# A ring of six value pages and a re-timed order of slots in a two-layer decoder's merged attention stage

## The reference, cut to what matters

```python
# prompt, one block of 128 queries
sc = einsum('bqhd,bkhd->bhqk', qi, k) * scale + ci[..., :, None] - c_k[:, :, None, :]
p = softmax(where(causal, sc, NEG_INF)); out = einsum('bhqk,bkhd->bqhd', p, v)
# sample
k_past = k_pool[page_table].reshape(bd, p_len, h, d)      # v_past, lf_past alike
s_past = einsum('bqhd,bkhd->bhqk', q, k_past) * scale + cq[..., :, None] + r_past
p = softmax(concatenate([s_past, s_new], -1))
out = einsum(p[..., :p_len], v_past) + einsum(p[..., p_len:], v)
```

## Time and profile before

| | us |
|---|---|
| median of 3 runs (lowest, highest) | 2018.95 (2005.68, 2023.38) |
| the profiled execution | 2022.65 |
| its span, first to last instruction | 2020.9 |
| merged stage in it, 1119.0 to 1519.3 | 400.3 |
| of which slots 4 to 27, 1165.4 to 1456.6 | 291.2 |

### The profile page before, as it was taken

How to read it: one execution, slowest core, us unless ns; L and a number is a source line. 1 busy time by engine, 2 the same in 40 slices (tenths; PEclk the granted TensorE clock), 3 DMA queues, 4 the chain that set the end, 5 groups by cost and what they waited for, 6 DMA issues and landing times.

```text
span 2020.9 us, 37879 instructions
## 1 busy us (share of the span) xinstructions
PE 1770.0 (88%) x15111; PEld 1542.6 (76%) x15111; DVE 942.3 (47%) x1367; ACT 561.5 (28%) x1008; POOL 111.4 (6%) x217
## 2 busy tenths in 40 slices
PE   5999565979999999899977687788779899999999
PEld 4876443979999999889954444444439799999998
DVE  5388776453333322467546755555523533333221
ACT  3210223232222211243332333433322322222211
POOL 1000000000000000144310000000000000000000
PEclk9999876999999999999977788888879899999999
DMA  3211031212222322223343677777772222222331
GB/s 118 60 46 32 21 100 42 82 54 83 83 83 80 88 87 86 66 68 79 80 149 98 220 237 246 270 252 254 248 245 69 62 83 83 83 82 82 95 101 53
DMA packets 240211, 224.87 MB, mean 111 GB/s; under 512 B 12290, under 2 KB 200340, under 8 KB 240090
## 3 DMA queue, kind: packets, MB, share of 16 engines
q1 hardware_dynamic: 229776, 201.13, 31.8%
q0 software_dynamic: 8896, 18.79, 3.1%
q10 hardware_dynamic: 1418, 3.29, 0.5%
HBM read 215.37 MB, written 7.80 MB: 110 GB/s over the span
## 4 chain that ended last, share of the span: by engine, by line
PE 76%; DVE 12%; DMA 4%; issue 3%; ACT 3%; SPq 2%; ACTq 0%; DVEq 0%; POOL 0%; POOLq 0%
PE ps L1490 56%; PE ps L1920 4%; DMA vring<-in_cache_fox_v_dram 4%; PE ps L1696 3%; PE ps L1965 2%; PE ps L1899 1%; DVE tmp L440 1%; PE ps L1472 1%; DVE yc L719 1%; SPq L2078 1%; DVE aL L444 1%; DVE rb L435 1%; DVE rb L450 1%; PE ps L1558 1%; PE ps L1881 1%
## 5 line engine op out<-in xcount | busy, mean ns | idle before, releaser
L1490 PE MATMUL ps<-aH,wH 128*128 128x288 f32 x2224 | 488.5, 302 | 49.1 <-DVE aL L444 33.5
L1490 PE MATMUL ps<-aL,wH 128*128 128x288 f32 x2224 | 481.4, 298 | 0.0
L1490 PE MATMUL ps<-aH,wL 128*128 128x288 f32 x2224 | 481.0, 298 | 0.0
L1490 PEld LDWEIGHTS ps<-aH,wH 128*128 128x128 f32 x2224 | 362.7, 191 | 58.0 <-issue 35.6
L421 DVE TENSOR_TENSOR wL<-raw,wH 128x1024 fp32r<-128x1024 f32 (+1 forms) x179 | 232.0, 1296 | 331.9 <-ACT wH L1046 328.8
L1490 PEld LDWEIGHTS ps<-aL,wH 128*128 128x128 f32 x2224 | 363.5, 191 | 0.0
L1490 PEld LDWEIGHTS ps<-aH,wL 128*128 128x128 f32 x2224 | 363.3, 191 | 0.0
L1046 ACT ACTIVATE wH<-raw 128x1024 fp32r<-128x1024 f32 (+1 forms) x179 | 198.9, 1111 | 381.4 <-PE ps L1490 352.2
L1490 PE MATMUL ps<-gH,wH 128*128 128x288 f32 x704 | 151.6, 296 | 0.0
L1490 PE MATMUL ps<-gH,wL 128*128 128x288 f32 x704 | 151.1, 295 | 0.0
L1490 PE MATMUL ps<-gL,wH 128*128 128x288 f32 x704 | 151.0, 295 | 0.0
(11 more groups left out here) (307 smaller groups left out, 1802.3 us busy)
## 6 DMA issues: line engine op xcount, KB each, us to landing
kset<-in_cache_fox_k_dram SPq DMA_DIRECT2D x128, 384.0 KB, 4.3
vring<-in_cache_fox_v_dram SPq DMA_DIRECT2D x128, 384.0 KB, 4.8
raw<-in_w_gate_up_dram SPq DMA_DIRECT2D x88, 512.0 KB, 3.8
raw<-in_w_down_dram SPq DMA_DIRECT2D x32, 704.0 KB, 4.6
raw<-in_fox_w_in_dram SPq DMA_DIRECT2D x21, 512.0 KB, 3.9
raw<-in_w_out_dram SPq DMA_DIRECT2D x16, 512.0 KB, 4.2
raw<-in_conv_w_in_dram SPq DMA_DIRECT2D x14, 512.0 KB, 3.8
raw<-in_w_mem_kv_dram SPq DMA_DIRECT2D x8, 512.0 KB, 3.7
```

What stands on the lines that cost most here:

```text
L1490: mm = nc.tensor.matmul(ps[:, 2 * slot + h, 0:HT], weights[:, w], a[:, k0 + k, h * HT:(h + 1) * HT], start=(first and k == 0 and weights i ...
```

## The change

It alters the merged stage alone. The ring holds six value pages in place of four; the room comes from the buffer qr, so that `spread` now copies straight from qkT, in 16 copies of 32 partitions in place of 4 of 128, and the 16 copies that filled qr ahead of the stage are left out. SP asks for a chunk of keys one slot later. Even slots take three value pages and odd slots five. A sample's transposed probabilities go through banks 0 to 3, which the scores have left, in place of four PT entries of banks 6 and 7; one semaphore (pt_ready) tells ACT of all of them, and the next `set_scores` waits for ACT's copies (pt_taken). On PE `set_scores` and two value pages come ahead of `step_probT`, and `step_values` comes after all of the slot's pages; `step_hi` and `step_lo` treat the step before the last. The two rows of keys' sums (ncb) are made in two slots.

```diff
-    VRING = 4
+    VRING = 6
...
-    TURNS = [("ncb", 0, 0), ("ncb", 0, 1)]
+    TURNS = [("ncb", 0, 0)]
     for s in range(SLOTS + SPB):
         b, cc = divmod(s, SPB)
         step = 1 <= s <= STEPS
-        TURNS += [("probT", s - 1)] if step else []
         if cc == 2 and s < SLOTS:
             TURNS += [("new", b)]
+        TURNS += [("probT", s - 1)] if step else []
         if cc == 1 and b >= 2:
             TURNS += [("out", b - 2)]
+        if s % 5 == 0 and s < STEPS:
+            TURNS += [("ncb", s // 5, 1)]
         TURNS += [("pv", s - 1)] if step else []
-        if cc == 3 and s < SLOTS:
-            TURNS += [("PT", b, g) for g in range(4)]
         if (s + 1) % 5 == 0 and s + 1 < STEPS:
-            TURNS += [("ncb", (s + 1) // 5, e) for e in range(2)]
+            TURNS += [("ncb", (s + 1) // 5, 0)]
...
-        qr, o = at("qr", [P, NH, 2, NS], o)
...
-                if k == 0:
-                    for n in range(2):
-                        wait_taken(dve, ("ncb", i // 5, n))
+                if k < 2:
+                    wait_taken(dve, ("ncb", i // 5, k))
...
                     step_sums(s)
+                if 2 <= s <= STEPS + 1:
+                    step_lo(s - 2)
...
-                if 1 <= s <= STEPS:
-                    step_lo(s - 1)
...
-            act.wait_ge(hn_done, Z + 1 + HP)
-            act.wait_ge(mL_done, KD)
-            for e in range(2):
-                for c in range(2):
-                    r = slice(DH * e + DQ * c, DH * e + DQ * c + DQ)
-                    for a in range(4):
-                        last = nc.scalar.activation(qr[DQ * a:DQ * a + DQ].rearrange("p (g e) c n -> p g e c n", e=2)[:, :, e, c, :],
-                                                    qkT[r, 0:HP, SEQ:T], ACT.Copy)
-            last.then_inc(qr_done, 1)
...
             def spread(b):
 
                 if b:
                     act.wait_ge(sc_done, 2 * b)
                     wait_turn(act, ("new", b - 1))
-                for m in range(4):
-                    nc.scalar.activation(qx4[:].rearrange("p (j m c) n -> p j m c n", m=4, c=2)[:, :, m, :, NQ * m:NQ * m + NQ],
-                                         qr[:].rearrange("p (j m) c n -> p j m c n", m=4)[:, :, m, :, NQ * b:NQ * b + NQ], ACT.Copy)
+                for e in range(2):
+                    for c in range(2):
+                        for a in range(4):
+                            rows = slice(DH * e + DQ * c, DH * e + DQ * c + DQ)
+                            mine = qx4[DQ * a:DQ * a + DQ, 2 * e + c, NQ * e:NQ * e + NQ]
+                            mine = bass.AP(tensor=mine.tensor, offset=mine.offset, ap=[mine.ap[0], [8 * QR, 3], [4 * QR + 2 * NQ, 2], [1, NQ]])
+                            nc.scalar.activation(mine, qkT[rows, 0:HP, SEQ + NQ * b:SEQ + NQ * b + NQ].rearrange("p (j m) q -> p j m q", m=2), ACT.Copy)
...
             def sample_probT(b):
 
-                for g in range(4):
-                    n = min(5, NP - 5 * g)
-                    bank = turn_bank(("PT", b, g))
-                    wait_turn(act, ("PT", b, g))
-                    last = nc.scalar.activation(pTs[:, 5 * g:5 * g + n, :].rearrange("p k r -> p (k r)"), bank[:, 0:n * ROWS], ACT.Copy)
-                    if g == 3:
-                        last = nc.scalar.activation(pTs[0:NS, NP, :], bank[0:NS, n * ROWS:(n + 1) * ROWS], ACT.Copy)
-                    last.then_inc(taken(("PT", b, g)), 1)
+                act.wait_ge(pt_ready, b + 1)
+                nc.scalar.activation(pTs[:, 0:15, :].rearrange("p (g k) r -> p g (k r)", g=3), ps[:, 0:3, 0:5 * ROWS], ACT.Copy)
+                nc.scalar.activation(pTs[:, 15, :], ps[:, 3, 0:ROWS], ACT.Copy)
+                nc.scalar.activation(pTs[0:NS, NP, :], ps[0:NS, 3, ROWS:2 * ROWS], ACT.Copy).then_inc(pt_taken, 1)
...
-            c_keys(0)
+            c_keys(0, 0)
             spread(0)
             for s in range(SLOTS + SPB):
                 b, cc = divmod(s, SPB)
-                if 1 <= s <= STEPS:
-                    step_probT(s - 1)
                 if cc == 0 and b >= 2:
                     sample_scale(b - 2)
+                if 2 <= s <= STEPS + 1:
+                    step_hi(s - 2)
                 if cc == 3 and b < NB:
                     sample_exp(b)
                 if s < STEPS:
                     step_exp(s)
+                if 1 <= s <= STEPS:
+                    step_probT(s - 1)
                 if cc == 1 and b >= 2:
                     sample_hi(b - 2)
-                if 1 <= s <= STEPS:
-                    step_hi(s - 1)
+                if s % 5 == 0 and s < STEPS:
+                    c_keys(s // 5, 1)
                 if cc == 3 and b < NB:
                     sample_probT(b)
...
-                        pe.wait_ge(sexp_done, b)
+                        pe.wait_ge(pt_taken, b)
...
             def sample_probT(b):
 
                 pe.wait_ge(sexp_done, b + 1)
-                for g in range(4):
-                    bank = turn(("PT", b, g))
-                    n = min(5, NP - 5 * g)
-                    for x in range(n):
-                        k = 5 * g + x
-                        mm = nc.tensor.transpose(bank[:, x * ROWS:(x + 1) * ROWS], S[:, k * P:(k + 1) * P], ident[0:ROWS, 0:ROWS])
-                    if g == 3:
-                        mm = nc.tensor.transpose(bank[0:NS, n * ROWS:(n + 1) * ROWS], S[:, NPAST:NPAST + NS], ident[0:ROWS, 0:ROWS])
-                    mm.then_inc(turn_ready, 1)
+                for k in range(NP):
+                    nc.tensor.transpose(ps[:, k // 5, k % 5 * ROWS:(k % 5 + 1) * ROWS], S[:, k * P:(k + 1) * P], ident[0:ROWS, 0:ROWS])
+                nc.tensor.transpose(ps[0:NS, 3, ROWS:2 * ROWS], S[:, NPAST:NPAST + NS], ident[0:ROWS, 0:ROWS]).then_inc(pt_ready, 1)
 
             def values(b, k):
 
                 n = NP * b + k
                 pe.wait_ge(v_in[n % VRING], 16 * (n // VRING + 1))
                 if k == 0:
-                    wait_taken(pe, ("PT", b, 3))
-                    wait_taken(pe, ("PT", b, 2))
+                    pe.wait_ge(pt_taken, b + 1)
...
                 step = 1 <= s <= STEPS
-                if step:
-                    step_probT(s - 1)
+                first = NP * cc // SPB + (0, -1, 0, -1)[cc]
+                last = NP * (cc + 1) // SPB + (-1, 0, -1, 0)[cc]
                 if s < SLOTS and cc % 2 == 0:
                     set_scores(2 * b + cc // 2)
                     if cc == 2:
                         new_scores(b)
                 if b:
-                    values(b - 1, 4 * cc)
-                    values(b - 1, 4 * cc + 1)
+                    for k in range(first, first + 2):
+                        values(b - 1, k)
+                if step:
+                    step_probT(s - 1)
                 if cc == 1 and b >= 2:
                     sample_out(b - 2)
+                if s % 5 == 0 and s < STEPS:
+                    c_keys(s // 5, 1)
+                if b:
+                    for k in range(first + 2, last):
+                        values(b - 1, k)
+                if cc == 3 and s < SLOTS:
+                    sample_probT(b)
                 if step:
                     step_values(s - 1)
-                if b:
-                    values(b - 1, 4 * cc + 2)
-                    values(b - 1, 4 * cc + 3)
-                if cc == 3 and s < SLOTS:
-                    sample_probT(b)
                 if (s + 1) % 5 == 0 and s + 1 < STEPS:
-                    c_keys((s + 1) // 5)
+                    c_keys((s + 1) // 5, 0)
...
-            for s in range(SLOTS + SPB - 1):
-                for n in (2 * s + NCH, 2 * s + NCH + 1):
-                    if n < NB * NCH:
+            for s in range(1, SLOTS + SPB):
+                for n in (2 * s + NCH - 2, 2 * s + NCH - 1):
+                    if NCH <= n < NB * NCH:
...
-                for n in range(4 * (s - 3), 4 * (s - 2)):
-                    if n >= VRING:
+                for n in range(4 * (s - 4) + VRING - s % 2, 4 * (s - 3) + VRING - (s + 1) % 2):
+                    if VRING <= n < NB * NP:
                         value_page(n)
```

More of the change, by code:

```diff
@@ L353, in build @@
         e_done, zab_done, c_ready, c_done, stage_done = (sem(n) for n in ("e_done", "zab_done", "c_ready", "c_done", "stage_done"))
-        lftot_done, qr_done, clear_done = (sem(n) for n in ("lftot_done", "qr_done", "clear_done"))
+        lftot_done, clear_done = (sem(n) for n in ("lftot_done", "clear_done"))
         turn_ready = sem("turn_ready")
@@ L360, in build @@
         smax_done, sexp_done, srec_done = (sem(n) for n in ("smax_done", "sexp_done", "srec_done"))
+        pt_ready, pt_taken = sem("pt_ready"), sem("pt_taken")
         o_ready, os_done, s_hi, v_used = (sem(n) for n in ("o_ready", "os_done", "s_hi", "v_used"))
@@ L1333, in _, with c_keys @@
             sample_memory(1, u + len(MEM_UNITS))
[L1335 to L1339, removed]
+            def c_keys(two, n):
+                wait_turn(act, ("ncb", two, n))
```

(6 more changed lines are left out.)

## The result

The changed kernel takes 2033.34 us in the median of 16 runs (2028.24 to 2038.43), the kernel before 2018.62 in 16 runs beside it (2005.68 to 2029.37). The ratio is 1.0068, interval 1.0053 to 1.0083: slower by 0.7%, where 0.2% faster was forecast.

What follows compares the result with a forecast made beforehand. PE waiting for value pages of an unevenly asked DMA was taken as the bound. A turn summed -10.7 + 6.1 + 0.8 + 2.7 + 1.0 = -0.1; with -4 in the tail this gave 2015 us, range 1972 to 2038.

Steps and rivals of the forecast that it cites:

- the clock's term: PE after waits: 1.7 us lost per slow stretch, but none new at set_scores of a sample's change, already at 0.50.
- the forecast's own case: Whole kernel: new waits offset those removed, 2015 us, 1998 to 2030; chance 0.53.
- a bare 4.7: Slot 15: step_probT waits for a bank and holds up the sample's transposes by 4.7 us, 0.8 a turn.
- The ring and the keys: PE's waits for value pages and their slow stretches go: 10.7 us a turn gained, at least 7.3.
- DVE's step_lo: Slot 1: os_ transposes wait for step_lo, PE idles 4.4 us, with slow clock 6.1 a turn.
- ACT's chain: From last transpose to set_scores: copies, step_scale and spread take 5.7 us, PE idles 3.6 instead of 0.9, 2.7 more a turn.
- the prediction's own sign of being wrong: Stated in advance: sample_out finds its bank free, the clock stays 1.00 through the waits, or spread is dearer than its forerunners.
- The issue term: Waits inside set_scores with no releaser: 1.0 us a turn added as the DMA gets busier, between nothing and 2.1.
- The tail: Last value pages: six in place, ten left at 1.15 us, 11.5 in place of 15.4; -4, at least -2.4.
- The first: Rival: new waits lie beside other work and bubbles close; 1951 to 1983 us, 1967 in the middle; chance 0.25.
- The second: Rival: spread's copies cost more and set_scores waits for all; 2059 us at 0.53 each, 2037 half way; chance 0.14.
- The third: Rival: the ring doesn't end the waits, keys stand ahead of values in one queue; 2047 us; chance 0.08.

Runs made afterwards that it cites:

- e7: Changed kernel with step_lo between step_top and keys_T on DVE, and spread's copies on POOL; 1957.63 us, 0.9676 of before.
- e6: Changed kernel with spread's copies done by POOL instead of ACT; 1993.42 us, 0.9865 of before.
- e1: Changed kernel with step_lo moved on DVE from behind keys_T to between step_top and keys_T; 2001.53 us, 0.9901 of before.
- e9: Kernel before with one edit in SP's list, a chunk of keys asked one slot later; 2010.98 us, 0.9915 of before.
- e10: Changed kernel with spread on POOL and step_lo ahead of step_top on DVE; 1957.76 us, 0.9664 of before.
- e12: e7 with keys asked as before the change, ring of six kept; 1981.30 us, 0.9833 of before.
- e14: e7 with four value pages in every slot and a ring of four; 1977.04 us, 0.9790 of before.
- e5: Kernel before with a ring of six value pages asked two ahead, no qr, spread in 16 copies; 2028.20 us, 1.0039 of before.
- e4: Kernel before without qr, spread in 16 copies straight from qkT, ring of four; 2058.50 us, 1.0165 of before.

## Why the prediction was wrong

**The step that failed is the clock's term, in the words that set_scores "already ran at clock 0.50 there, so no new stretch".** The 2033 lies inside the range, but above the 1998 to 2030 of the forecast's own case, and the change went the other way. The sum for six turns was about 0: idle time 6 x (-7.3 + 4.4 + 0.8 + 2.7 + 1.0) = 9.6 us more, and slow stretches 6 x (-2 + 1) x 1.7 = 10.2 us less. Measured are 12.0 us more idle time and 0.2 us less of PE's busy time. So 10.0 of the 12.4 us by which the six turns missed are the clock.

Rows 4 show one set_scores at a sample's change, that of slot 28, at 0.50. Rows 7 show another, 3.90 us at 1408.05, which is the full clock, and I used only its start. These are windows with set_scores alone at the six changes of slots 4 to 24 (window, PE busy in set_scores, its clock, DMA share, GB/s): two of the kernel before and the sum of its six, then one and the sum of the changed kernel, then the sum of e7.

```profile
1165.30:1174.30 9.00, 6.34 (x192) 0.74 0.12 24
1408.00:1417.00 9.00, 4.10 (x192) 1.00 0.51 170
sum 54.00, PE 28.53; mean PE 4.75
```

```profile
1416.20:1425.20 9.00, 6.68 (x192) 0.69 0.48 168
sum 54.00, PE 39.05; mean PE 6.51
```

```profile
sum 54.00, PE 24.68; mean PE 4.11
```

Before, four of the six ran at 1.00; behind the wait for spread all six take 6.37 to 6.68 us. That is 10.5 us more, where I had put nothing. Everything else that PE does in the six turns became 10.7 us shorter, and 10.2 were forecast for it. With spread on POOL the wait is gone, and five of the six run at 1.00 in e6 (26.4 us), all six in e7 (24.7); e1, which keeps the wait, stays at 38.4. In slot 15 I made the same mistake with a bare 4.7: 5.3 us of waiting, then 11.4 at half clock, 4.8 lost (already taken off those 10.7).

That the idle time was sized to 2.4 us is partly luck. DVE's waits came to 2.4 more than forecast and ACT's chain to 6.6 more (28.2 with step_values' wait, against 21.6), while 6.0 were added to the gaps in set_scores, which grew by nothing.

Idle time taken away often gives the clock back: from the changed kernel to e1, e6 and e7, 20.2, 19.4 and 45.2 us less idle time went with 5.8, 9.6 and 18.7 less of PE's busy time. It isn't a rate to count on: from before to e9 idle time fell by 23.7 us and PE's busy time grew by 8.5, and from e7 to e10 by 4.3 and 4.2. In e9 7.0 of the 8.5 stand again in set_scores at the changes (35.5), shortly after the new waits of L1950, the sample's transposes; what it is in e10 was not tried.

**The ring and the keys**: the mechanism was right, the waits fell to none; with the new waits taken away (e7) a turn is 8.7 us shorter than before, forecast 7.3 to 10.7. But it was put down to both together, and e9, e12 and e14 show that the later keys do the larger part. The Trainium skill ("Perfetto Trace Analysis", Optimization Strategy) says that a repeated gap can mean too few buffers. The runs agree by half: six buffers with the old order of asking still waited 16.4 (e5) and 11.6 us (e12), four with the new one 6.2 (e9).

**DVE's step_lo**: right in kind and size. os_ waits 4.4 each time. It happened four times, not six, in the six turns; I had seen slot 15 but not that slots 5 and 25 wait in the same way. Together 33.5 us, forecast 31.1.

**ACT's chain**: the copy of 1440 took 1.37 (forecast 1.45) and step_scale 0.90, as forecast; spread's copies stand 0.25 apart, not 0.135, as they don't overlap as the four did. PE idled 4.3 for spread and 0.75 in step_values at a change, 5.0 in place of 3.6. This is the prediction's own sign of being wrong, spread dearer than its four forerunners. Rows 9 held the answer: sixteen copies of that form stood 0.53 apart, and each of them is 0.51 to 0.53 long in the trace, so they didn't overlap either; sixteen of the 0.24 that I took for one are 3.9. The Trainium skill ("ScalarE: Activation LUTs", What ACT_TABLE_LOAD costs) gives 186 ns plus 0.833 ns an element for such an instruction, and an overlap of 93 ns between neighbours, measured on tiles of 128 partitions; for 48 elements that would be an estimate of 0.13 apart. The trace agrees for the four copies of 128 partitions (0.135); for the sixteen of 32 it shows the length (0.22 to 0.24) but no overlap, and by the measurement they take 3.99.

**The issue term**: of the 14.7 us in the changed kernel, 3.1 (1368.86) and 2.1 (1164.45, ahead of the window) stand ahead of set_scores and are waits for spread as well, which leaves 9.5 inside it. Of the 12.4 before, 1.9 stand ahead of it too (four times some 0.5, as in rows 7), so I had misread where they lie. Inside, 10.5 became 9.5: my 1.0 a turn was not there, although the DMA was busier in slot 0's set_scores (0.60 to 0.66 in four of six, at most 0.39 before).

**The tail**: -0.3, forecast -4. PE's timeline after:

```profile
1507.29 1.07 PE L1948 MATMUL ps<-vring,pTs 128*32 128x256 f32 x6 [2.17 <-ACT os__144 L1401]
1508.87 3.01 PE L1948 MATMUL ps<-vring,pTs 128*32 128x256 f32 x18 [0.51 <-DMA vring<-in_cache_fox_v_dram]
...
1524.07 1.04 PE L1948 MATMUL ps<-vring,pTs 128*32 128x256 f32 x6 [0.53 <-DMA vring<-in_cache_fox_v_dram]
```

From the second page on, 14 intervals take 15.2 us, 1.1 each: the pace of a full DMA that I had worked out. But I had put six pages in place at the start, and PE waits from the second on.

**The rivals.** The first, "bubbles simply close", gave 1951 to 1983: the price was right (e7: 1957.6), but only once step_lo and spread had been moved. The second had its mechanism right (spread's copies cost more than the four's, and set_scores waits for all of them); at 0.25 a copy its own formula gives 13 us, 2028. That 2033 lies near its half-way price of 2037 is not by that price: the clock behind the wait makes up the rest. The third is ruled out by the waits for pages.

## What to carry over

When a wait is removed, ask of every engine what it now finishes last, and in which place of its list the short instruction stands that the next one needs: step_lo, 0.3 us long, stood behind 3.4 us of other work, and moving it ahead ended 28 of the 38 us that PE waited for it. Price an idle stretch of PE with its clock, new ones as well as old ones, and look at every place where it will stand: one window at half clock didn't speak for the other changes of sample. The busy time in the windows shows whether the clock was gained. And before a buffer is given up for room, ask which chain the copies in its place will end, and whether an idle engine can do them: the later keys cost one line, and the room for the ring was paid with sixteen copies.

## What was not expected of the hardware

The sixteen copies of 32 partitions don't overlap on ACT: they stand 0.25 us apart, where four copies of 128 partitions and as many elements stood 0.135 apart. Twelve of the sixteen go to other partitions and four stay on their own, and all stand equally far apart; what keeps them apart was not tried. POOL, made to wait for each copy, did the same sixteen in 4.41 us, against ACT's 3.99. The gaps inside set_scores without a releaser stay at 7 to 15 us in six turns in all kernels, whatever the DMA's share (0.64 to 0.90); what they are was not tried and stays open. The rows of such waits also count waits ahead of set_scores: of e4's 27.8 us, 15.9 are four waits for spread.
